# The gate stage of a two-block network: high and low halves of four matmul units side by side in PSUM, and the scaling moved to GpSimd

## The chip, the cores and the metric

The kernel runs on one core of a Trainium2 chip. One program computes the whole network in one launch. The metric is the device time of one execution in microseconds (us). An execution carries five instruction streams that meet only at semaphores: TensorE (PE, matmul and weight load), VectorE (DVE), ScalarE (ACT), GpSimd (POOL) and SyncE (SP, which here only issues DMAs).

## The reference, cut to what matters

The network is two blocks of two layers each, on 256 tokens of width 1024, all in float32. The change lies in the first mixer of the first layer, a gated MLP:

```python
def gmlp_mixer(x, w_in, ln_g, ln_b, w_s, b_s, w_out):
    B, S, _ = x.shape
    z = jax.nn.gelu(x @ w_in)
    u, v = z[..., :GMLP_WIDTH], z[..., GMLP_WIDTH:]
    v = layernorm(v, ln_g, ln_b)
    v = v.reshape(B, S // GMLP_CHUNK, GMLP_CHUNK, GMLP_GROUPS, GMLP_GROUP_DIM)
    ...
    v = jnp.einsum('gpq,bnqgc->bnpgc', ws, v) + b_s.T[None, None, :, :, None]
    return (u * v.reshape(B, S, GMLP_WIDTH)) @ w_out

    y = rmsnorm(h, norm_g[layer, 0])
    y = gmlp_mixer(y, ...)
    h = h + rmsnorm(y, norm_g[layer, 1])
    y = rmsnorm(h, norm_g[layer, 2])
    y = conv_ffn(y, ...)
```

The first RMS norm is applied late: the matmuls run on the unscaled input, and their results are multiplied by the token's `rs2` (one over the root mean square) afterwards.

## The kernel before

**Tiling.** All weights come as units of 128 x 2048 floats (1 MB), in the order in which they are used. SP loads unit u into slot u % 3 of `raw`, as soon as the low part of unit u-3 is made. Each unit is split in two: ACT copies it to a rounded high part `w_hi` (`split_hi`, 2048 columns), and DVE subtracts that from the raw unit and leaves the low part `w_lo` (`split_lo`). Activations are held in the same two parts, `a_hi` and `a_lo`, side by side in `a_hl`. A product is the sum of three matmuls: high x high, high weight x low activation, low weight x high activation.

**The stage.** Units 0 to 3 make v (token-major, in the `acc` banks of PSUM), units 4 to 7 make u (feature-major, each unit two tiles of 128 features x 256 tokens, in the `wk` banks), units 8 to 11 are the output projection (into `wk` again). The four units of u are numbered q = 0 to 3 below. On PE the order is: unit 3, u units q = 0, 1, 2, then `spatial` (the einsum with w_s), then q = 3, then unit 8, whose second token half may write banks 2 and 3 of `wk` only once the last unit of u has been read out of them (`last_bank`), then units 9 to 11 (`last_downs`).

**How a u unit runs.** `unit_feat` (L693) issues for each of 8 slices and 2 feature tiles the three matmuls of `three` (L687 to L691), all of 256 columns, into one PSUM bank: 48 matmuls. It starts when the low weights are there. DVE's `scale_u(q)` (L2030) multiplies that bank by `rs2` into `uT`, ACT's `gelu_u(q)` (L1500) applies gelu to `uT` in place, and DVE's `gate(b)` (L2034) adds the spatial bias to a bank of `acc` (L2039) and multiplies by `uT` (L2044). ACT's `gate_high` and DVE's `gate_low` make the high and low parts `b_hi`, `b_lo` for the projection. Elsewhere in the kernel a second form of unit exists: `unit_pair` (L706), which streams `a_hl` as 512 columns (high and low activations side by side) past the high weights, two banks wide, 16 matmuls, and then `low_pair` (L754), 16 matmuls of 256 columns with the low weights. There ACT copies the low halves of the two banks to SBUF (L1542) and DVE adds the high halves to them (L2079).

**What sets the order.** Every engine's order is written out by hand. DVE's order in this stage is `norm_v` (layer norm of v, with `split_lo` of unit 6 in it), then three times `scale_u` with `split_lo` of units 7 and 8 between, then the gates, `split_lo` of unit 9, `scale_u(3)` and the rest. POOL has nothing to compute in the stage: after a memset it waits until unit 4 is done and loads the two gain rows (`load_gains`, L572) that DVE multiplies by in the stage that follows (L1795). After the stage POOL takes part in the FFN's gating: `gate_first` (L393, both inputs in SBUF) and `gate_second` (L401).

Of the kernel before, what the change touches and what calls it, by code (L numbers as in the profile page):

```python
# [122 lines left out]
def build(nc, xT, x_rows, gains, cols, rows, ws, wsT, rel_bias, pool_w, onehot, line_dram, lines_dram, out):  # L123
    ctx = ExitStack()
    with ctx:
# [146 lines left out]
        v_gelu, u_scaled, u_gelu = sem("v_gelu"), sem("u_scaled"), sem("u_gelu")  # L272
# [18 lines left out]
        d_low, s_low = sem("d_low"), sem("s_low")  # L291
# [12 lines left out]
                ("pad_zero", "low", "padded", "tap2", "taps", "gelu", "gated", "hid_hi", "hid_lo", "last_gated", "last_lo")} for l in range(2)]  # L304
# [247 lines left out]
        def _(pool):  # L552
# [133 lines left out]
        def _(pe):  # L686
# [1777 lines left out]
```

## Time and profile before

| what | value |
|---|---|
| time, median of 3 runs | 1054.45 us (1054.29 to 1055.08) |
| the profiled execution's own time | 1055.49 us |
| its span, first to last instruction | 1053.8 us |
| PE busy in the span | 1044.0 us (99%) |
| DVE busy | 783.9 us (74%) |
| ACT busy | 614.5 us (58%) |
| POOL busy | 119.2 us (11%) |
| the changed stage in the span | about 31 to 81 us |

The profiled execution is 1.0 us above the median, and 1.7 us of it lie outside the span. Matmuls are pipelined, so that records overlap: a 512-column matmul is recorded with 0.39 us, but the next one starts 0.23 us later. Costs of PE are therefore read from start to start. DVE's records overlap a little too (0.69 us recorded for a 512-column addition, the next starts after 0.60 us).

### The profile page before, as it was taken

What the parts mean: (1) busy time and instruction counts of PE and PEld (TensorE: products, weight loads), DVE (VectorE), ACT (ScalarE), POOL (GpSimd) and SP (SyncE); (2) the same over time, 40 slices, a digit from 0 to 9 for tenths busy, and PEclk for the clock granted to TensorE, in tenths of its full rate; (3) what the DMA queues carried; (4) which work ended last, traced back from release to release, by engine and by line L of the source; (5) the groups of instructions that cost most, each with busy time, mean ns of one, the idle gap of its engine ahead of it and who ended that gap; (6) DMA issues with size and microseconds to landing.
All of it is one profiled execution on the core that took longest, in us unless ns stands there. A gap on an engine that the chain in (4) does not pass through costs nothing.

```text
span 1053.8 us, 15320 instructions
## 1 busy us (share of the span) xinstructions
PE 1044.0 (99%) x6158; PEld 919.5 (87%) x6158; DVE 783.9 (74%) x960; ACT 614.5 (58%) x846; POOL 119.2 (11%) x117
## 2 busy tenths in 40 slices
PE   9999999999999999999999999999999999999997
PEld 7989888888999898888888988888899989888886
DVE  6979877676888799788868856556878869655654
ACT  6757666557666676665766535344566666434442
POOL 0000431220000004753110000000000000000000
PEclk9999999999999999999999999999999999999999
DMA  8944885554445447756551564555354435665551
GB/s 312 346 156 173 285 302 170 190 203 157 165 157 198 160 159 242 266 187 236 171 200 40 208 249 163 204 196 173 147 208 153 138 105 198 221 211 187 184 175 40
DMA packets 31750, 201.17 MB, mean 191 GB/s; under 512 B 3736, under 2 KB 4416, under 8 KB 9408
## 3 DMA queue, kind: packets, MB, share of 16 engines
q1 hardware_dynamic: 28608, 188.12, 50.4%
q0 software_dynamic: 3072, 12.07, 3.5%
q8 instruction: 49, 0.80, 0.3%
q14 instruction: 21, 0.17, 0.0%
HBM read 199.12 MB, written 2.63 MB: 191 GB/s over the span
## 4 chain that ended last, share of the span: by engine, by line
PE 92%; DVE 3%; DMA 2%; ACT 1%; issue 1%; SPq 0%; DVEq 0%; ACTq 0%
PE wk L713 22%; PE wk L761 15%; PE acc L689 9%; PE acc L690 9%; PE acc L691 9%; PE wk L689 5%; PE wk L691 5%; PE wk L690 5%; PE wk L742 4%; PE wk L831 2%; DMA raw<-ws 2%; PE acc L742 2%; PE acc L761 1%; PE acc L927 1%; PE acc L1213 0%
## 5 line engine op out<-in xcount | busy, mean ns | idle before, releaser
L354 DVE TENSOR_TENSOR w_lo<-raw,w_hi 128x2048 fp32r<-128x2048 f32 x159 | 365.5, 2303 | 46.2 <-ACT w_hi L333 41.2
L333 ACT ACTIVATE w_hi<-raw 128x2048 fp32r<-128x2048 f32 x165 | 314.5, 1908 | 9.7 <-DMA raw<-ws 7.2
L713 PE MATMUL wk<-a_hl,w_hi 128*128 128x512 f32 x1024 | 243.2, 390 | 0.0
L713 PEld LDWEIGHTS wk<-a_hl,w_hi 128*128 128x128 f32 x1024 | 190.6, 188 | 38.5
L761 PEld LDWEIGHTS wk<-a_hl,w_lo 128*128 128x128 f32 x1296 | 165.3, 191 | 5.5
L689 PE MATMUL acc<-w_hi,b_hl 128*128 128x512 f32 x432 | 168.9, 391 | 0.0
L690 PE MATMUL acc<-w_lo,b_hl 128*128 128x512 f32 x432 | 168.6, 390 | 0.0
L691 PE MATMUL acc<-w_hi,b_hl 128*128 128x512 f32 x432 | 168.1, 389 | 0.0
L761 PE MATMUL wk<-a_hl,w_lo 128*128 128x256 f32 (+1 forms) x1296 | 168.0, 283 | 0.0
L1687 ACT ACTIVATE region<-wk 128x512 f32<-128x512 f32 x30 | 17.9, 596 | 158.1 <-PE wk L761 158.1
L691 PEld LDWEIGHTS acc<-w_hi,b_hl 128*128 128x128 f32 x432 | 81.1, 188 | 17.2
L689 PEld LDWEIGHTS acc<-w_hi,b_hl 128*128 128x128 f32 x432 | 81.3, 188 | 15.7
L690 PEld LDWEIGHTS acc<-w_lo,b_hl 128*128 128x128 f32 x432 | 81.3, 188 | 15.2
L2262 DVE TENSOR_TENSOR region<-wk,region 128x512 f32<-128x512 f32 x30 | 20.7, 691 | 92.8 <-ACT region L1687 92.8
L2089 DVE SCALAR_TENSOR_TENSOR region<-region,prm 128x256 f32<-128x256 f32 x176 | 82.0, 508 | 7.2 <-ACT region L1554 5.7
L393 POOL TENSOR_TENSOR region<-region 128x512 f32<-128x512 f32 x20 | 50.7, 2537 | 233.2 <-ACT region L1583 233.2
L1542 ACT ACTIVATE region<-wk 128x512 f32<-128x512 f32 x42 | 25.0, 594 | 73.5 <-PE wk L761 73.5
L1554 ACT ACTIVATE region<-region,prm 128x256 f32<-128x256 f32 x88 | 47.7, 590 | 8.5 <-DVE region L2079 8.5
L2079 DVE TENSOR_TENSOR region<-wk,region 128x512 f32<-128x512 f32 x42 | 28.8, 687 | 28.1 <-ACT region L1542 28.0
L1350 ACT ACTIVATE b_hl<-region 128x512 fp32r<-128x512 f32 x58 | 36.0, 623 | 22.3 <-POOL region L393 9.2
L578 POOL DMA_DIRECT2D gain<-gains x12 | 6.9, 577 | 371.0 <-ACT region L1477 183.1
L742 PE MATMUL wk<-a_hl,w_hi 128*128 128x256 f32 x352 | 45.4, 284 | 0.9 <-DVE a_hl L1887 0.8
(287 smaller groups left out, 1538.9 us busy)
## 6 DMA issues: line engine op xcount, KB each, us to landing
raw<-ws SPq DMA_DIRECT2D x171, 1024.0 KB, 4.9
gain<-gains POOLq DMA_DIRECT2D x12, 512.0 KB, 6.0
raw<-ws SPq DMA_DIRECT2D x12, 256.0 KB, 6.6
region<-rows SPq DMA_DIRECT2D x1, 1664.0 KB, 10.9
lines_dram<-line_dram POOLq DMA_DIRECT2D x1, 1536.0 KB, 8.2
bias<-gains POOLq DMA_DIRECT2D x3, 512.0 KB, 8.1
region<-xT SPq DMA_DIRECT2D x4, 256.0 KB, 6.4
x<-x_rows SPq DMA_DIRECT2D x1, 1024.0 KB, 9.2
```

The costliest lines, as they stand in the source:

```text
L333: act.activation(high_of(u), raw[:, u % RAW, :], ACT.Copy).then_inc(hi_ready, 1)
L354: dve.tensor_tensor(low_of(u), raw[:, u % RAW, :], high_of(u).bitcast(F32), ALU.subtract).then_inc(lo_ready, 1)
L393: eng.tensor_tensor(hf[:, p:p + 2, :], gl[:, p:p + 2, :], cv[:, p:p + 2, 1, :], ALU.mult)\
L689: pe.matmul(o, still, moving, start=first, stop=False, skip_group_check=True)
L690: pe.matmul(o, still, moving_lo, start=False, stop=False, skip_group_check=True)
L691: return pe.matmul(o, still_lo, moving, start=False, stop=last, skip_group_check=True)
L713: pe.matmul(banks[:, m, :], wh[:, k, m * P:(m + 1) * P], a_hl[:, k, :, :].rearrange("p e t -> p (e t)"), start=k == 0, stop=False, skip_gr ...
L742: pe.matmul(banks[:, m, :].rearrange("p (e t) -> p e t", e=2)[:, :, c], wh[:, k, m * P:(m + 1) * P], a_hl[:, k, :, c], start=h == 0 and k ...
L761: mm = pe.matmul(banks[:, m, T + c.start:2 * T], wl[:, k, m * P:(m + 1) * P], hi[:, k, c], start=False, stop=k == DT - 1, skip_group_check ...
L1350: act.activation(dst, src, ACT.Copy, **kw).then_inc(done, 1)
L1554: act.activation(cv[:, p + a, q, :], hb[:, p + a, q, 2:HW], ACT.Identity, scale=w, bias=bb)\
L2089: dve.scalar_tensor_tensor(out=cv[:, p + a, q, :], in0=hb[:, p + a, q, tap:tap + T], scalar=prm[:, bass.ds(col, 1)], in1=cv[:, p + a, q, : ...
```

## The change

Each u unit now runs as `unit_pair`: 16 matmuls of 512 columns and 16 of 256 instead of 48 of 256. The results lie in two half banks: the first 256 columns of each of two banks hold the products with the high activations and with the low weights, the other 256 those with the low activations. Units q = 0 and 2 use banks 0 and 1 of `wk`, q = 1 and 3 banks 2 and 3, so that q = 2 and 3 have to wait until q = 0 and 1 are read out. ACT copies the low halves into `gain`, which serves as scratch (`copy_u`), DVE adds the high halves to them into `uT` (`sum_u`), and the multiplication by `rs2` becomes an instruction of its own on `uT` in SBUF: on POOL for q = 0 to 2, on DVE for q = 3. The two gain rows are loaded only when the scratch is free, after the fourth sum. In `norm_v`, `split_lo` of unit 6 moves between the first two instructions, and `split_lo` of units 7 and 8 follow the second and the third sum. ACT's copies are placed between its splits, and `gate_high` of bank 0 comes ahead of `gelu_u(2)`. Renamed semaphores elsewhere change no order.

```diff
+        def u_banks(q):
+            return wk[:, 2 * (q % 2):2 * (q % 2) + 2, :]
+
+        def u_copied(q):
+            return two(gain[:, q % 2, 0:2 * T])
...
             pool.memset(wst[HD:P, :, 0:HD], 0.0).then_inc(wst_masked, 1)
-            pool.wait_ge(unit_done, U_GMLP + 5)
+            pool.wait_ge(wst_masked, 1)
+            pool.wait_ge(rs2_ready, 1)
+            for q in range(3):
+                pool.wait_ge(u_summed, q + 1)
+                pool.tensor_tensor(uT[:, 2 * q:2 * q + 2, :], uT[:, 2 * q:2 * q + 2, :], rs2_two, ALU.mult).then_inc(u_scaled, 1)
+            pool.wait_ge(u_summed, 4)
             load_gains(J_GMLP)
...
             for q in range(4):
-                if q == 2:
+                if q == 1:
                     pe.wait_ge(line_copied, 1)
-                if q == 3:
                     pe.wait_ge(sd2_ready, 1)
-                unit_feat(U_GMLP + 4 + q, q)
+                elif q >= 2:
+                    pe.wait_ge(u_summed, q - 1)
+                unit_pair(U_GMLP + 4 + q, u_banks(q))
...
             pe.wait_ge(gate_lo, 1)
-            unit_down(U_GMLP + 8, *b_pair(0), True, res=wk, last_bank=(u_scaled, 4))
+            pe.wait_ge(u_summed, 3)
+            unit_down(U_GMLP + 8, *b_pair(0), True, res=wk, last_bank=(u_summed, 4))
...
+            act.wait_ge(unit_done, U_GMLP + 5)
+            act.activation(u_copied(0), u_banks(0)[:, :, T:2 * T], ACT.Copy).then_inc(u_low, 1)
             split_hi(act, U_GMLP + 3 + CUT)
...
+            def copy_u(q):
+                act.wait_ge(unit_done, U_GMLP + 4 + q + 1)
+                act.activation(u_copied(q), u_banks(q)[:, :, T:2 * T], ACT.Copy).then_inc(u_low, 1)
...
-            for q in range(3):
-                split_hi(act, U_GMLP + 4 + q + CUT)
-                gelu_u(q)
-            for b in range(3):
-                gate_high(b)
+            copy_u(1)
+            split_hi(act, U_GMLP + 4 + CUT)
+            gelu_u(0)
+            split_hi(act, U_GMLP + 5 + CUT)
+            copy_u(2)
+            gelu_u(1)
+            split_hi(act, U_GMLP + 6 + CUT)
+            gate_high(0)
+            gelu_u(2)
+            gate_high(1)
+            gate_high(2)
+            copy_u(3)
             split_hi(act, U_GMLP + 7 + CUT)
             gelu_u(3)
...
-                split_lo(dve, U_GMLP + 3 + CUT)
+                    if n == 0:
+                        split_lo(dve, U_GMLP + 3 + CUT)
...
-            def scale_u(q):
-                dve.wait_ge(unit_done, U_GMLP + 4 + q + 1)
-                dve.tensor_tensor(uT[:, 2 * q:2 * q + 2, :], two(wk[:, q, :]), rs2_two, ALU.mult).then_inc(u_scaled, 1)
+            def sum_u(q):
+                dve.wait_ge(u_low, q + 1)
+                dve.tensor_tensor(uT[:, 2 * q:2 * q + 2, :], u_banks(q)[:, :, 0:T], u_copied(q), ALU.add).then_inc(u_summed, 1)
...
+            sum_u(0)
             norm_v()
-            for q in range(3):
-                scale_u(q)
-                if q < 2:
-                    split_lo(dve, U_GMLP + 4 + q + CUT)
+            for q in range(1, 3):
+                sum_u(q)
+                split_lo(dve, U_GMLP + 3 + q + CUT)
             gate(0)
...
             split_lo(dve, U_GMLP + 6 + CUT)
-            scale_u(3)
+            sum_u(3)
+            dve.wait_ge(u_summed, 4)
+            dve.wait_ge(u_scaled, 3)
+            dve.tensor_tensor(uT[:, 6:8, :], uT[:, 6:8, :], rs2_two, ALU.mult).then_inc(u_scaled, 1)
             gate_low(2)
```

VectorE from the layer norm of v to the first gate, before (L2032 is `scale_u`, L354 `split_lo`; `region` holds `uT` and v):

```order
L2012 SCALAR_TENSOR_TENSOR region<-region 128x1024 [waits row_landed,ln_step]
L2012 SCALAR_TENSOR_TENSOR region<-region 128x1024
L354 TENSOR_TENSOR w_lo<-raw,w_hi 128x2048 [waits unit_done,hi_ready]
L2017 RECIPROCAL region<-region 128x2 [waits ln_sd_ready]
L2020 SCALAR_TENSOR_TENSOR region<-region 128x1024 [waits ln_step]
L2020 SCALAR_TENSOR_TENSOR region<-region 128x1024
L2032 TENSOR_TENSOR region<-wk,region 128x512 [waits unit_done]
L354 TENSOR_TENSOR w_lo<-raw,w_hi 128x2048 [waits unit_done,hi_ready]
L2032 TENSOR_TENSOR region<-wk,region 128x512 [waits unit_done]
L354 TENSOR_TENSOR w_lo<-raw,w_hi 128x2048 [waits unit_done,hi_ready]
L2032 TENSOR_TENSOR region<-wk,region 128x512 [waits unit_done]
L2039 TENSOR_TENSOR bias<-acc,region 128x512 [waits spatial_done]
```

VectorE at the same place after the change (L2061 is `sum_u`, L356 `split_lo`; `gain` is the scratch):

```order
L2061 TENSOR_TENSOR region<-wk,gain 128x512 [waits u_low]
L2040 SCALAR_TENSOR_TENSOR region<-region 128x1024 [waits row_landed,ln_step]
L356 TENSOR_TENSOR w_lo<-raw,w_hi 128x2048 [waits unit_done,hi_ready]
L2040 SCALAR_TENSOR_TENSOR region<-region 128x1024
L2046 RECIPROCAL region<-region 128x2 [waits ln_sd_ready]
L2049 SCALAR_TENSOR_TENSOR region<-region 128x1024 [waits ln_step]
L2049 SCALAR_TENSOR_TENSOR region<-region 128x1024
L2061 TENSOR_TENSOR region<-wk,gain 128x512 [waits u_low]
L356 TENSOR_TENSOR w_lo<-raw,w_hi 128x2048 [waits unit_done,hi_ready]
L2061 TENSOR_TENSOR region<-wk,gain 128x512 [waits u_low]
L356 TENSOR_TENSOR w_lo<-raw,w_hi 128x2048 [waits unit_done,hi_ready]
L2068 TENSOR_TENSOR bias<-acc,region 128x512 [waits spatial_done]
```

The first sum stands ahead of the layer norm, each sum waits for ACT's copy instead of for PE, and the number of instructions up to the first gate is the same.

GpSimd from its constants to its first gating instruction, before:

```order
L569 MEMSET minus_half 128x4
L583 MEMSET region 64x8x64 [waits row_landed,consts_set]
L578 DMA gain<-gains 128x1024 [waits unit_done]
L578 DMA gain<-gains 128x1024
L393 TENSOR_TENSOR region<-region 128x512 [waits ffn0_gelu,ffn0_taps]
```

GpSimd after the change (L596 is the scaling, L586 `load_gains`):

```order
L577 MEMSET minus_half 128x4
L591 MEMSET region 64x8x64 [waits row_landed,consts_set]
L596 TENSOR_TENSOR region<-region 128x512 [waits u_summed,rs2_ready,wst_masked]
L596 TENSOR_TENSOR region<-region 128x512 [waits u_summed] x2
L586 DMA gain<-gains 128x1024 [waits u_summed]
L586 DMA gain<-gains 128x1024
```

Three multiplications with both inputs in SBUF stand ahead of the gain loads, and the loads wait for the fourth sum instead of for unit 4.

## Rows read from the trace of the kernel before

**Rows 1.** The page: busy time, share and instructions; the chain by engine.

```profile
PE 1044.0 (99%) x6158; PEld 919.5 (87%) x6158; DVE 783.9 (74%) x960; ACT 614.5 (58%) x846; POOL 119.2 (11%) x117
PE 92%; DVE 3%; DMA 2%; ACT 1%; issue 1%; SPq 0%; DVEq 0%; ACTq 0%
```

**Rows 2.** Timeline of PE, 31 to 62: start us, us, engine, line, operation, [idle before].

```profile
31.22 0.39 PE L691 MATMUL acc<-w_hi,a_hl 128*128 128x512 f32 x1
31.75 0.38 PE L689 MATMUL wk<-a_hl,w_hi 128*128 128x256 f32 x1
31.97 0.28 PE L690 MATMUL wk<-a_hl,w_hi 128*128 128x256 f32 x1
32.09 0.28 PE L691 MATMUL wk<-a_hl,w_lo 128*128 128x256 f32 x1
...
49.12 3.73 PE L980 MATMUL acc<-region 128*128 128x128 f32 x32
52.61 0.36 PE L689 MATMUL wk<-a_hl,w_hi 128*128 128x256 f32 x1
...
58.44 0.40 PE L689 MATMUL wk<-w_hi,b_hl 128*128 128x512 f32 x1
...
61.19 0.39 PE L689 MATMUL wk<-w_hi,b_hl 128*128 128x512 f32 x1
```

**Rows 3.** Timeline of VectorE, 29 to 60, same columns.

```profile
29.40 2.29 DVE L354 TENSOR_TENSOR w_lo<-raw,w_hi 128x2048 fp32r<-128x2048 f32 x1
...
38.01 2.48 DVE L2012 SCALAR_TENSOR_TENSOR region<-region 128x1024 f32<-128x1024 f32 x2
...
45.20 0.69 DVE L2032 TENSOR_TENSOR region<-wk,region 128x512 f32<-128x512 f32 x1
45.80 2.29 DVE L354 TENSOR_TENSOR w_lo<-raw,w_hi 128x2048 fp32r<-128x2048 f32 x1
...
53.51 0.69 DVE L2049 TENSOR_TENSOR b_hl<-bias,b_hl 128x512 fp32r<-128x512 f32 x1 [0.70 <-ACT b_hl L1350]
...
59.58 0.68 DVE L2032 TENSOR_TENSOR region<-wk,region 128x512 f32<-128x512 f32 x1
```

**Rows 4.** Timeline of PE, 99.6 to 106: one unit in pair form, and the next one's start.

```profile
99.66 3.82 PE L713 MATMUL wk<-a_hl,w_hi 128*128 128x512 f32 x16
103.32 2.08 PE L761 MATMUL wk<-a_hl,w_lo 128*128 128x256 f32 x16
105.23 1.09 PE L713 MATMUL wk<-a_hl,w_hi 128*128 128x512 f32 x4
```

**Rows 5.** The page's groups of the copy and the sum: xcount | busy, mean ns | idle before.

```profile
L1542 ACT ACTIVATE region<-wk 128x512 f32<-128x512 f32 x42 | 25.0, 594 | 73.5 <-PE wk L761 73.5
L2079 DVE TENSOR_TENSOR region<-wk,region 128x512 f32<-128x512 f32 x42 | 28.8, 687 | 28.1 <-ACT region L1542 28.0
```

**Rows 6.** Timelines of GpSimd and VectorE where both work: at 103, 432 and 462.

```profile
103.23 1.29 POOL L393 TENSOR_TENSOR region<-region 128x512 f32<-128x512 f32 x1 [63.92 <-ACT region L1583]
103.49 3.18 DVE L354 TENSOR_TENSOR w_lo<-raw,w_hi 128x2048 fp32r<-128x2048 f32 x1
...
432.51 2.55 POOL L393 TENSOR_TENSOR region<-region 128x512 f32<-128x512 f32 x1 [1.09 <-ACT region L1583]
431.62 2.28 DVE L354 TENSOR_TENSOR w_lo<-raw,w_hi 128x2048 fp32r<-128x2048 f32 x1
433.83 0.68 DVE L2079 TENSOR_TENSOR region<-wk,region 128x512 f32<-128x512 f32 x1
...
462.54 2.54 POOL L393 TENSOR_TENSOR region<-region 128x512 f32<-128x512 f32 x1 [7.49 <-ACT region L1583]
461.65 2.29 DVE L354 TENSOR_TENSOR w_lo<-raw,w_hi 128x2048 fp32r<-128x2048 f32 x1
463.85 2.39 DVE L2130 TENSOR_TENSOR o_lo_t<-region,o_hi_t 128x512 fp32r<-128x512 f32 x2
```

**Rows 7.** GpSimd's gain loads (line L578: issue to landing), and VectorE's first use of them.

```profile
DMA to landing us min/median/max: 4.4/6.0/10.8
71.73 0.15 DVE L1792 TENSOR_SCALAR ss_eps<-ss 128x1 f32<-128x1 f32 x1 [4.01 <-ACT region L1382]
```

**Rows 8.** Stretches at the span's end: us, PE, PEld, DVE, ACT, POOL busy (x), PEclk, DMA.

```profile
1040.00:1048.00 8.00, 7.95 (x36) 6.24 (x34) 2.84 (x7) 1.51 (x6) 0.00 (x0) 1.00 0.18 66
1048.00:1051.00 3.00, 0.00 (x0) 0.00 (x0) 2.36 (x7) 0.97 (x3) 0.00 (x0) 1.00 0.04 15
1051.00:1053.80 2.80, 0.00 (x0) 0.00 (x0) 0.17 (x1) 0.00 (x0) 0.00 (x0) 0.51 0.52 172
```

More of the change, by code:

```diff
@@ L270, in build @@
         out_stored = sem("out_stored")
-        v_gelu, u_scaled, u_gelu = sem("v_gelu"), sem("u_scaled"), sem("u_gelu")
+        v_gelu, u_low, u_summed, u_scaled, u_gelu = (
+            sem("v_gelu"), sem("u_low"), sem("u_summed"), sem("u_scaled"), sem("u_gelu"))
         ln_step, ln_sd_ready, spatial_done = sem("ln_step"), sem("ln_sd_ready"), sem("spatial_done")
@@ L289, in build @@
             sem("o_hi"), sem("o_lo"), sem("sub_ready"))
-        d_low, s_low = sem("d_low"), sem("s_low")
+        qk_low = sem("qk_low")
+        pad_zero = sem("pad_zero")
         sq_ready, sk_ready, sv_ready = sem("sq_ready"), sem("sk_ready"), sem("sv_ready")
@@ L303, in build @@
         ffn = [{n: sem(f"ffn{l}_{n}") for n in
-                ("pad_zero", "low", "padded", "tap2", "taps", "gelu", "gated", "hid_hi", "hid_lo", "last_gated", "last_lo")} for l in range(2)]
+                ("low", "padded", "tap2", "taps", "gelu", "gated", "hid_hi", "hid_lo", "last_gated", "last_lo")} for l in range(2)]
         mlp = [{n: sem(f"mlp{l}_{n}") for n in
@@ L1637, in diff_outputs @@
                     part(2 * j + 1)
-            low_copy(U_DIFF, wk[:, 0:2, :], diff_low[:, 0, :, :], d_low)
+            low_copy(U_DIFF, wk[:, 0:2, :], diff_low[:, 0, :, :], qk_low)
             split_hi(act, U_DIFF + 3)
-            low_copy(U_DIFF + 1, wk[:, 2:4, :], diff_low[:, 1, :, :], d_low)
+            low_copy(U_DIFF + 1, wk[:, 2:4, :], diff_low[:, 1, :, :], qk_low)
             split_hi(act, U_DIFF + 4)
@@ L1728, in _ @@
             act.preload_act_table_set("natural_log_exp_and_others")
-            low_copy(U_STICK, wk[:, 0:2, :], stick_low[:, 0, :, :], s_low)
+            low_copy(U_STICK, wk[:, 0:2, :], stick_low[:, 0, :, :], qk_low)
             split_hi(act, U_STICK + 3)
-            low_copy(U_STICK + 1, wk[:, 2:4, :], stick_low[:, 1, :, :], s_low)
+            low_copy(U_STICK + 1, wk[:, 2:4, :], stick_low[:, 1, :, :], qk_low)
             split_hi(act, U_STICK + 4)
             act.wait_ge(sq_ready, 1)
-            low_copy(U_STICK + 2, acc[:, 2:4, :], stick_low[:, 0, :, :], s_low)
+            low_copy(U_STICK + 2, acc[:, 2:4, :], stick_low[:, 0, :, :], qk_low)
             split_hi(act, U_STICK + 5)
@@ L2133, in ffn_phase @@
             def ffn_phase(l, base, n):
-                dve.memset(hb[:, :, :, 0:2], 0.0).then_inc(ffn[l]["pad_zero"], 1)
-                dve.wait_ge(ffn[l]["pad_zero"], 1)
+                dve.memset(hb[:, :, :, 0:2], 0.0).then_inc(pad_zero, 1)
+                dve.wait_ge(pad_zero, l + 1)
                 for i in range(FI):
@@ L2210, in _ @@
             dve.wait_ge(lam_step, 5)
-            feat_sum(wk[:, 0:2, :], diff_low[:, 0, :, :], d_low, 1, qT[:, 0:2, :], dq_ready)
+            feat_sum(wk[:, 0:2, :], diff_low[:, 0, :, :], qk_low, 1, qT[:, 0:2, :], dq_ready)
             split_lo(dve, U_DIFF + 3)
-            feat_sum(wk[:, 2:4, :], diff_low[:, 1, :, :], d_low, 2, kT[:, 0:2, :], dk_ready)
+            feat_sum(wk[:, 2:4, :], diff_low[:, 1, :, :], qk_low, 2, kT[:, 0:2, :], dk_ready)
             diff_bias(0)
@@ L2332, in stick_rest @@
                     stick_low_part(t)
-            feat_sum(wk[:, 0:2, :], stick_low[:, 0, :, :], s_low, 1, qT[:, 0:2, :], sq_ready)
+            feat_sum(wk[:, 0:2, :], stick_low[:, 0, :, :], qk_low, 3, qT[:, 0:2, :], sq_ready)
             split_lo(dve, U_STICK + 3)
-            feat_sum(wk[:, 2:4, :], stick_low[:, 1, :, :], s_low, 2, qT[:, 2:4, :], sq_ready)
-            feat_sum(acc[:, 2:4, :], stick_low[:, 0, :, :], s_low, 3, qT[:, 4:6, :], sq_ready)
+            feat_sum(wk[:, 2:4, :], stick_low[:, 1, :, :], qk_low, 4, qT[:, 2:4, :], sq_ready)
+            feat_sum(acc[:, 2:4, :], stick_low[:, 0, :, :], qk_low, 5, qT[:, 4:6, :], sq_ready)
             for c in range(3, 12):
```

## The prediction

> **What bounds the kernel now.** I read the page first: PE is busy for 1044.0 of 1053.8 us, and 92% of the chain that ended last is PE [rows 1]. Whatever PE gains in a stage is therefore kept, unless PE then waits, and whatever PE waits for in a stage is lost. So I went to PE's timeline of the stage: it has no gap between 31.75 and 81, apart from one at its start. The last matmul of unit 3 starts at 31.22 and, at the 0.23 us from start to start of 512-column matmuls, the next could have started at 31.45; the first u unit starts at 31.75, right behind DVE's low part of unit 4, which ends at 29.40 + 2.29 = 31.69 [rows 2, 3]. Then I laid DVE's timeline beside it, because the change hangs PE on DVE more closely. DVE is just as full: from 38.01, where the layer norm of v begins, to 60.26, where the last scaling ends (59.58 + 0.68), it has one idle stretch of note, 0.70 us ahead of the first `gate_low` [rows 3]. PE needs that last scaling for the second half of unit 8, which starts at 61.19 [rows 2], so DVE is only 0.93 us early there. This is the place where the change is decided.
>
> **PE's part.** A u unit in the old form is 48 matmuls at 0.12 us from start to start [rows 2], 5.76 us. In the pair form the trace shows one unit from 99.66 to the next one's start at 105.23, 5.57 us [rows 4]. That is 0.19 us a unit, 0.76 us for four. The pair form waits for the high weights only, which were there long before, so the gap of 0.30 us at 31.45 goes as well, and with it the slow restart of the first matmul (0.22 us to the next instead of 0.12). In sum PE arrives earlier by 0.76 + 0.30 + 0.10, about 1.2 us. Laid out: q = 0 from 31.45, q = 1 from 37.0, q = 2 from 42.6, `spatial` from 48.2 (3.49 us as before, 49.12 to 52.61 [rows 2]), q = 3 from 51.7, unit 8 from 57.2 instead of 58.44, and its second half would start 2.75 us later (58.44 to 61.19), at 60.0.
>
> **ACT's part.** Four copies are added, 0.59 us each [rows 5]. They stand on ACT's queue, which has room in this stage; the first of them waits for unit 4 until 37.2 and pushes `split_hi` of unit 6 from 35.2 to 37.7, so DVE's `split_lo` of it may start from 39.7, which is about where DVE arrives. The last copy stands behind `gate_high(2)`, and can be done by 59.9 by the layout below; DVE asks for it at 61.5. I cost ACT at nothing; without that cover the fourth copy's 0.59 us would come on top.
>
> **DVE's part without GpSimd.** `scale_u` (0.69 us) becomes `sum_u` (0.69 us [rows 5]); the first of them moves ahead of the layer norm, where ACT's copy is done at 37.8, just before DVE is free at 38.0. The multiplication for q = 3 (0.6 us) is added, but behind the fourth sum, which is what PE waits for. So up to the end of the fourth sum DVE has the same work as before, and would end it at 60.26.
>
> **GpSimd's three multiplications.** Here the trace of before has a close relative: L393, the same 128x512 multiplication of float32 in SBUF. Alone it takes 1.29 us, but beside DVE's `split_lo` 2.54 us [rows 6]. At 462.54 it begins while a `split_lo` runs, and ends at 465.08, 1.14 us behind that instruction's end (461.65 + 2.29 = 463.94). DVE's next instruction, also with two SBUF inputs, is held: two of them take 2.39 us from 463.85, where two take about 1.29. At 103.23 GpSimd was first, and the `split_lo` took 3.18 us instead of 2.29. So GpSimd waits for the instruction that DVE has under way, and then DVE's next instruction with two SBUF inputs waits for GpSimd, up to 1.1 us. An addition with one input in PSUM is not held: 0.68 us at 433.83, while GpSimd was still at work until 435.06 [rows 6].
>
> The Trainium skill's page "GPSIMD Engine Reference", section "Key points", says that GpSimd shares its SBUF interfaces with VectorE and contends with instructions that have two SBUF inputs. By that rule `sum_u` and the first half of a gate, which read PSUM, go free, and the trace agrees with its 0.68 us.
>
> Each multiplication is released by the sum in front, and DVE is fully loaded behind each:
> - The first waits for the first layer-norm instruction (to 39.8) and holds `split_lo` of unit 6 until 41.0: 1.10 us lost.
> - The second waits for `split_lo` of unit 7 (to 49.7) and holds until 50.9. DVE spends 0.60 us of that on the third sum, which goes free; `split_lo` of unit 8 loses about 0.50.
> - The third waits for `split_lo` of unit 8 (to 53.0) and holds until 54.2. The gate's PSUM half goes free, its SBUF half loses about 0.35.
>
> Together 1.95 us. The fourth sum starts at 59.58 + 1.95 = 61.5 and ends at 62.2.
>
> **The sum.** PE stands at unit 8's second half from 60.0 and goes on at 62.28 (0.06 us behind DVE, as at 31.69 to 31.75), with 0.08 us of restart. Before, this half started at 61.19. The stage is later by 62.28 + 0.08 - 61.19, some 1.1 us: PE's 1.2 us are gone, and 1.1 more. What follows on PE has its inputs: `split_lo` of units 9, 10 and 11 ends at 61.5, 67.0 and 69.8, PE wants them at 65.1, 67.8 and 70.5. From there all moves together, since the next stage begins with this one's result.
>
> The span becomes 1053.8 + 1.1 = 1054.9, that execution's own time 1055.49 + 1.1 = 1056.6, and the median 1054.45 + 1.1 = 1055.5 us.
>
> **The gain rows.** They are issued at about 62.3 and 62.9 instead of 38. At the median landing of 6.0 us they are there at 69, at the maximum of 10.8 at 73.7; DVE first needs them at 71.73 + 1.1 = 72.8, after 4 us of idleness [rows 7]. I take the median: nothing; the other end is 0.9 us.
>
> **Rivals.**
> - *GpSimd gives way* (its multiplications find gaps, or DVE is held for less than the rows show). The fourth sum ends at 60.26, PE goes on at 60.32 + 0.08 and the stage is 0.8 us earlier: 1053.65. For it speaks only that the scaling's second input is a broadcast row, which L393 has not; against it three collisions in [rows 6].
> - *GpSimd holds every DVE instruction*, sums and PSUM halves too, so that each of the three costs 1.1 us: 3.3 us. The fourth sum ends at 63.6, PE goes on at 63.6 + 0.14, the stage is 2.5 us later: 1056.95, slower by more than 0.2%. It decides from 3.0 us of hold in all on. Against it speaks the 0.68 us row. The same time would come of a multiplication that takes 0.5 us longer with the broadcast row.
> - *The gains land late*: 0.4 to 0.9 us on top of the forecast, 1056.2.
> - *The clock*. PE's wait of 2.3 us would be the longest inside the span. At the tail the granted clock was still 1.00 in the first 3 us without a matmul, and fell to 0.51 on average (1.2 GHz) in the last 2.8 us [rows 8]. So the forecast's wait should leave it; a wait over 3 us, as in the second rival, might not: three us of work at half speed after it would be 1.5 us on top of that rival, 1058.5.
> - *The fourth copy or the wait for q = 0's sum holds PE*: both have over 1 us of slack in the layout, and count for nothing here.
>
> **How the numbers follow.** The forecast has 0.70, GpSimd giving way 0.15, holding everything 0.08, late gains 0.05, a fallen clock 0.02. A measurement of this kernel can tell about 0.2%, 2.1 us, from no change. The forecast, the first and the third rival lie within that (0.90, less 0.01 for a part of the first that goes further); the second and the fourth lie above (0.10 together). Range: the first rival's 1053.65 less 0.35 for the spread of the runs, to the second's 1056.95: 1053.3 to 1057.0.
>
> **What would show it.** After the change, PE should start u units at about 31.45, 37.0, 42.6 and 51.7, and wait some 2.3 us ahead of unit 8's second half for DVE's fourth sum. GpSimd's three multiplications should be recorded with about 2.3, 3.3 and 3.3 us, and of DVE's instructions `split_lo` of unit 6 with 3.4, of unit 8 with 2.8 and the first gate's second half with 1.0 us, against 2.29, 2.29 and 0.69. The prediction is wrong in its main step if these are recorded at their old lengths, or if PE waits elsewhere in the stage.

## The result, and the profile after

The changed kernel takes 1057.49 us in the median (before, on the same chip: 1054.52); the ratio is 1.0027, with a 95% interval of 1.0018 to 1.0036. Run again beside the kernel before, it took 1057.67 against 1054.67: 1.0023 (1.0013 to 1.0033). So it is slower by a quarter of a percent. The forecast was 1055.5, and its range ended at 1057.0.

The nine times of the second measurement are the first clue, because they fall into two groups: 1055.37, 1055.67 and 1055.85, then 1057.29 to 1058.50 (six). The lower group is the forecast's time.

Two of the nine times of the first measurement, 1284.14 and 1473.05 us, come from executions whose mean granted clock was 0.75 and 0.65; the ratio leaves them out (the median of the other seven is 1057.42 us), and since the profile of that measurement is of the first of them, the profiles below are from three later executions of the changed kernel. They took 1057.29 us (called X), 1055.57 (Y) and 1057.61 (Z): one of the lower group and two of the upper.

On the page of X the answers to [rows 1] show hardly a change. PE's busy time is 0.2 us less, POOL's 8.8 more, and the chain has gained one percent of DVE.

```profile
PE 1043.8 (99%) x6094; PEld 916.9 (87%) x6094; DVE 786.5 (75%) x961; ACT 616.7 (58%) x850; POOL 128.0 (12%) x120
PE 92%; DVE 4%; issue 1%; ACT 1%; DMA 1%; SPq 0%; DVEq 0%; ACTq 0%
```

PE's timeline of Y, the answer to [rows 2] (start, length, line, [idle before]):

```profile
30.68 3.79 PE L726 MATMUL wk<-a_hl,w_hi 128*128 128x512 f32 x16
...
36.22 3.82 PE L726 MATMUL wk<-a_hl,w_hi 128*128 128x512 f32 x16
...
41.78 3.82 PE L726 MATMUL wk<-a_hl,w_hi 128*128 128x512 f32 x16
...
59.00 0.39 PE L704 MATMUL wk<-w_hi,b_hl 128*128 128x512 f32 x1
61.31 0.50 PE L702 MATMUL wk<-w_hi,b_hl 128*128 128x512 f32 x1 [1.92 <-DVE region L2061]
```

The units of u are 5.54 and 5.56 us apart, as forecast (5.57), and PE's one wait in the stage is where it was forecast: ahead of unit 8's second half, for the fourth sum. From start to start PE is ready at 59.00 + 0.23 = 59.23 and goes on at 61.31, 2.08 us later; the forecast said 2.3.

DVE's and GpSimd's timelines of Y, the answers to [rows 3] and [rows 6]:

```profile
38.86 3.37 DVE L356 TENSOR_TENSOR w_lo<-raw,w_hi 128x2048 fp32r<-128x2048 f32 x1
...
46.54 2.28 DVE L356 TENSOR_TENSOR w_lo<-raw,w_hi 128x2048 fp32r<-128x2048 f32 x1
48.74 0.68 DVE L2061 TENSOR_TENSOR region<-wk,gain 128x512 f32<-128x512 f32 x1
49.34 2.76 DVE L356 TENSOR_TENSOR w_lo<-raw,w_hi 128x2048 fp32r<-128x2048 f32 x1
52.02 0.68 DVE L2068 TENSOR_TENSOR bias<-acc,region 128x512 f32<-128x512 f32 x1
52.73 1.07 DVE L2073 TENSOR_TENSOR bias<-bias,region 128x512 f32<-128x512 f32 x1
...
60.57 0.69 DVE L2061 TENSOR_TENSOR region<-wk,gain 128x512 f32<-128x512 f32 x1
```

```profile
37.92 2.16 POOL L596 TENSOR_TENSOR region<-region 128x512 f32<-128x512 f32 x1 [8.72 <-DVE region L2061]
46.70 6.55 POOL L596 TENSOR_TENSOR region<-region 128x512 f32<-128x512 f32 x2 [6.62 <-DVE region L2061]
```

The three holds are there at the forecast's sizes: `split_lo` of unit 6 at 3.37 us, of unit 8 at 2.76, the first gate's SBUF half at 1.07, while the third sum and the gate's PSUM half go free at 0.68.

The windows show where Y and X part. The columns are those of [rows 8]; the third from the end is the granted clock. Y:

```profile
61.00:62.00 1.00, 0.69 (x3) 0.60 (x4) 0.96 (x3) 0.00 (x0) 0.44 (x1) 1.00 0.86 139
62.00:63.00 1.00, 1.00 (x6) 0.82 (x5) 1.00 (x2) 0.99 (x2) 0.84 (x2) 1.00 0.55 197
63.00:64.00 1.00, 1.00 (x6) 0.81 (x5) 0.97 (x3) 1.00 (x1) 0.00 (x0) 1.00 1.01 426
```

X:

```profile
61.00:62.00 1.00, 0.61 (x3) 0.51 (x4) 0.96 (x3) 0.00 (x0) 0.36 (x1) 1.00 0.85 131
62.00:63.00 1.00, 1.00 (x5) 0.79 (x4) 1.00 (x3) 0.91 (x2) 0.92 (x2) 0.87 0.50 147
63.00:64.00 1.00, 1.00 (x4) 0.78 (x3) 0.96 (x3) 1.00 (x1) 0.00 (x0) 0.50 0.93 393
64.00:65.00 1.00, 1.00 (x4) 0.81 (x3) 1.00 (x1) 1.00 (x2) 0.00 (x0) 0.50 0.94 389
65.00:66.00 1.00, 1.00 (x3) 0.72 (x3) 1.00 (x1) 0.98 (x2) 0.00 (x0) 0.50 0.57 184
66.00:67.00 1.00, 1.00 (x5) 0.83 (x4) 1.00 (x3) 0.99 (x3) 0.00 (x0) 0.92 0.80 262
```

In X the granted clock falls to 0.50 (1.2 of 2.4 GHz) behind the wait and stays there until it rises again between 66 and 67. PE's timeline of X shows the same in its matmuls:

```profile
61.39 0.50 PE L702 MATMUL wk<-w_hi,b_hl 128*128 128x512 f32 x1 [1.92 <-DVE region L2061]
...
62.44 0.40 PE L703 MATMUL wk<-w_lo,b_hl 128*128 128x512 f32 x1
62.67 0.55 PE L704 MATMUL wk<-w_hi,b_hl 128*128 128x512 f32 x1
63.02 0.63 PE L702 MATMUL wk<-w_hi,b_hl 128*128 128x512 f32 x1
63.45 0.63 PE L703 MATMUL wk<-w_lo,b_hl 128*128 128x512 f32 x1
```

PE is back at work at 61.39, and the first slow matmul starts at 62.67; from 63.02 on they start 0.43 us apart instead of 0.23. The wait in front of it is 1.92 us in X and in Y. They are the same code, with the same holds and the same wait, and X is 1.72 us longer.

### The profile page after: what moved, and what is told of

Its sections match the earlier page's. It is cut to its first block, busy times and chain, and to the rows that moved or that the text cites. A ratio compares the mean times of both kernels' runs of the same rounds, so it can differ in the third digit from the quotient of the medians.

```text
span 1282.4 us, 15203 instructions
## 1 busy us (share of the span) xinstructions
PE 1274.5 (99%) x6094; PEld 1016.8 (79%) x6094; DVE 793.0 (62%) x961; ACT 617.2 (48%) x850; POOL 132.4 (10%) x120
## 4 chain that ended last, share of the span: by engine, by line
PE 99%; DVE 0%; ACT 0%; issue 0%; DVEq 0%; POOL 0%; POOLq 0%
PE wk L726 24%; PE wk L774 15%; PE acc L704 11%; PE acc L702 10%; PE acc L703 10%; PE wk L704 4%; PE wk L702 4%; PE wk L755 4%; PE wk L703 4%; PE wk L844 2%; PE acc L755 2%; PE acc L774 1%; PE acc L940 1%; PE wk L964 0%; PE wk L947 0%; PE acc L1228 0%
## 5 line engine op out<-in xcount | busy, mean ns | idle before, releaser
L356 DVE TENSOR_TENSOR w_lo<-raw,w_hi 128x2048 fp32r<-128x2048 f32 x159 | 366.7, 2310 | 96.9 <-ACT w_hi L335 50.8
L726 PE MATMUL wk<-a_hl,w_hi 128*128 128x512 f32 x1088 | 320.2, 456 | 0.0
L726 PEld LDWEIGHTS wk<-a_hl,w_hi 128*128 128x128 f32 x1088 | 215.4, 200 | 86.4
L774 PEld LDWEIGHTS wk<-a_hl,w_lo 128*128 128x128 f32 x1360 | 203.3, 212 | 13.1
L774 PE MATMUL wk<-a_hl,w_lo 128*128 128x256 f32 (+1 forms) x1360 | 207.7, 314 | 0.0
L702 PE MATMUL acc<-w_hi,b_hl 128*128 128x512 f32 x432 | 197.4, 457 | 0.0
L703 PE MATMUL acc<-w_lo,b_hl 128*128 128x512 f32 x432 | 197.1, 456 | 0.0
L704 PE MATMUL acc<-w_hi,b_hl 128*128 128x512 f32 x432 | 196.9, 456 | 0.0
L704 PEld LDWEIGHTS acc<-w_hi,b_hl 128*128 128x128 f32 x432 | 86.1, 199 | 35.5
L703 PEld LDWEIGHTS acc<-w_lo,b_hl 128*128 128x128 f32 x432 | 86.8, 201 | 33.2
L702 PEld LDWEIGHTS acc<-w_hi,b_hl 128*128 128x128 f32 x432 | 86.1, 199 | 33.2
L395 POOL TENSOR_TENSOR region<-region 128x512 f32<-128x512 f32 x20 | 57.4, 2872 | 244.7 <-ACT region L1611 244.7
L755 PE MATMUL wk<-a_hl,w_hi 128*128 128x256 f32 x352 | 52.9, 314 | 0.7 <-DVE a_hl L1915 0.7
L586 POOL DMA_DIRECT2D gain<-gains x12 | 7.0, 582 | 446.9 <-ACT region L1492 224.7
L755 PEld LDWEIGHTS wk<-a_hl,w_hi 128*128 128x128 f32 x352 | 51.5, 217 | 1.8 <-issue 1.0
```

Of the source, the lines that this page charges most:

```text
L356: dve.tensor_tensor(low_of(u), raw[:, u % RAW, :], high_of(u).bitcast(F32), ALU.subtract).then_inc(lo_ready, 1)
L395: eng.tensor_tensor(hf[:, p:p + 2, :], gl[:, p:p + 2, :], cv[:, p:p + 2, 1, :], ALU.mult)\
L702: pe.matmul(o, still, moving, start=first, stop=False, skip_group_check=True)
L703: pe.matmul(o, still, moving_lo, start=False, stop=False, skip_group_check=True)
L704: return pe.matmul(o, still_lo, moving, start=False, stop=last, skip_group_check=True)
L726: pe.matmul(banks[:, m, :], wh[:, k, m * P:(m + 1) * P], a_hl[:, k, :, :].rearrange("p e t -> p (e t)"), start=k == 0, stop=False, skip_gr ...
```

## The experiments

Three theories stood against each other. **A**: the three holds cost the forecast's 1 us, and the second group of times is chance that has nothing to do with the change. **B**: the wait that they make lets the clock fall, in a part of the executions. **C**: the longer times come from the chip of the first measurement, not from the kernel.

**The changed kernel again** (label e1_after; no edit).

> The changed kernel once more, for a profile at full clock. Theory A (the stage alone): three holds of GpSimd add 1.95 us to VectorE's chain, PE waits 2.3 us ahead of unit 8's second half, and the time is 1.1 us above before, with a mean granted clock of 0.999 as before. Theory B (the wait brings the clock down): in part of the executions PE's granted clock falls to 1.2 GHz for some us behind that wait; the mean clock is then 0.998 to 0.995 and the time 1 to 4 us above theory A's, differently from run to run. Theory C (the chip of that measurement): the low mean clocks have nothing to do with the kernel; before shows them on this chip too, or after shows none.

Measured: the second measurement above. Theory C falls, since the kernel before ran at 1054.67 beside it, and both kinds of times came from one chip.

**Without GpSimd's multiplications** (e2_no_pool). Three quarters of u are then not scaled.

```diff
                 pool.wait_ge(u_summed, q + 1)
-                pool.tensor_tensor(uT[:, 2 * q:2 * q + 2, :], uT[:, 2 * q:2 * q + 2, :], rs2_two, ALU.mult).then_inc(u_scaled, 1)
+                pool.memset(minus_half[:, q:q + 1], -0.5).then_inc(u_scaled, 1)
```

> The changed kernel with GpSimd's three multiplications left out (u is not scaled by rs2 for its first six tiles; a 128x1 memset counts the semaphore instead). Theories A and B: no hold, the fourth sum ends at 60.3 in the span, PE waits 0.3 us ahead of unit 8's second half, and the time is 0.8 us below before with a clock of 0.999 in every run. Theory C: 0.8 us below before plus whatever the chip's clock takes, as much as in the changed kernel.

Measured: 1054.50 us (1054.00 to 1054.67 in 11 runs, one group), ratio 0.9997 (0.9988 to 1.0006). DVE's timeline has all lengths back:

```profile
38.87 2.29 DVE L356 TENSOR_TENSOR w_lo<-raw,w_hi 128x2048 fp32r<-128x2048 f32 x1
...
48.19 0.69 DVE L2061 TENSOR_TENSOR region<-wk,gain 128x512 f32<-128x512 f32 x1 [0.45 <-ACT gain L1519]
48.80 2.28 DVE L356 TENSOR_TENSOR w_lo<-raw,w_hi 128x2048 fp32r<-128x2048 f32 x1
...
59.18 0.68 DVE L2061 TENSOR_TENSOR region<-wk,gain 128x512 f32<-128x512 f32 x1
```

The `split_lo` of unit 6 starts at the same time as in execution Y, so the fourth sums can be compared: 59.18 here, 60.57 there, 1.39 us. That is the holds' 1.94 less 0.55 us, most of it the 0.45 that DVE now waits for ACT's third copy. The second group of times goes when the multiplications go, and so does the 1 us. But against the kernel before only 0.17 us is won, not 0.8; PE still waits here:

```profile
59.92 0.50 PE L702 MATMUL wk<-w_hi,b_hl 128*128 128x512 f32 x1 [0.52 <-DVE region L2061]
```

**The wait filled** (e3_filled). PE multiplies a constant tile in the time in which it would wait; the delay stays, the idleness goes.

```diff
                     if last_bank is not None and h == 1:
+                        keep_warm(acc[:, 0, 0:T], filled)
                         pe.wait_ge(*last_bank)
...
-            unit_down(U_GMLP + 8, *b_pair(0), True, res=wk, last_bank=(u_summed, 4))
+            unit_down(U_GMLP + 8, *b_pair(0), True, res=wk, last_bank=(u_summed, 4), filled=16)
```

> The changed kernel with 16 matmuls of 256 bf16 columns on constants, into a bank that is free, between the two halves of unit 8: PE is at work for some 1.9 of the 2.3 us in which it waits. The holds stay. Theory A: time as the changed kernel, 1.1 us above before. Theory B: no drop of the clock, 0.999 in every run, 1.1 us above before while the changed kernel is 2 to 5 us above. Theory C: the same spread of clock and time as the changed kernel.

Measured: 1055.76 us (1055.49 to 1056.45 in 11 runs, one group), ratio 1.0011 (1.0002 to 1.0020). The holds are those of Y (3.37, 2.77, 1.07 us) and PE goes on at 61.12, nearly as late as in Y. PE's timeline:

```profile
59.03 1.92 PE L965 MATMUL acc<-warm 128*128 128x256 bf16 x16
61.12 0.50 PE L702 MATMUL wk<-w_hi,b_hl 128*128 128x512 f32 x1 [0.16 <-DVE region L2062]
```

Useless work of PE makes the changed kernel 1.9 us faster in the median. This is what theory B demands and theory A excludes.

**The wait alone, in the kernel before** (e4_before_late; e7_before_late2 with 256 in place of 1024 columns in the second addition). DVE gets two idle additions ahead of the last scaling; nothing of the change is in these kernels.

```diff
             split_lo(dve, U_GMLP + 6 + CUT)
+            for idle, n in ((o_lo_t, 2048), (o_hi_t, 1024)):
+                dve.tensor_tensor(idle[:, 0:n // T, :], row[:, 0:n].rearrange("p (k t) -> p k t", t=T), row[:, 0:n].rearrange("p (k t) -> p k t", t=T), ALU.add)
             scale_u(3)
```

> The kernel before with two idle additions on VectorE (2048 and 1024 columns, 3.35 us) ahead of the last scaling, which is what PE waits for at unit 8's second half: PE waits some 2.5 us there, without pair form, without GpSimd. Theories A and C: 2.5 us above before, clock 0.999. Theory B: 2.5 us plus a drop of the clock in part of the runs, so 3.5 to 6.5 us above before, with a mean clock of 0.998 to 0.995 and a spread of 1 us or more.

> The kernel before with two idle VectorE additions of 2048 and 256 columns ahead of its last scaling of u, so that TensorE waits about 1.9 us at unit 8's second half, as in the changed kernel, with GpSimd idle there. Theory B: times in two groups, about 1056.7 without a fall of the clock and 1058.4 with one, granted clock at 0.50 for some 3 us after the wait in the latter. Theory A: 1056.7 in every run, full clock.

Measured, e4: 1057.53, 1057.53, 1058.29, 1058.85, 1058.86. Its profiled execution is one of the two fastest, with a wait of 2.74 us and a clock of 1.00 behind it:

```profile
63.30 0.50 PE L689 MATMUL wk<-w_hi,b_hl 128*128 128x512 f32 x1 [2.74 <-DVE region L2032]
```

e7: 1056.61, 1056.83 and 1056.93, one at 1057.64, then 1058.38 to 1059.09 (four). Its profiled execution is the slowest; the wait is 1.90 us, and the clock is at 0.50 right behind it:

```profile
63.22 0.64 PE L689 MATMUL wk<-w_hi,b_hl 128*128 128x512 f32 x1 [1.90 <-DVE region L2032]
```

```profile
63.00:64.00 1.00, 0.78 (x2) 0.67 (x3) 1.00 (x3) 0.81 (x2) 0.00 (x0) 0.71 0.97 410
64.00:65.00 1.00, 1.00 (x4) 0.73 (x3) 0.96 (x2) 1.00 (x1) 0.00 (x0) 0.50 0.14 57
```

So a wait of 1.90 us was followed by a fall of the clock without GpSimd at work and without pair units; by the grouping of the times, not in every execution.

**The same, filled** (e8_late_filled: e4 and 22 of the matmuls of e3).

```diff
-            unit_down(U_GMLP + 8, *b_pair(0), True, res=wk, last_bank=(u_scaled, 4))
+            unit_down(U_GMLP + 8, *b_pair(0), True, res=wk, last_bank=(u_scaled, 4), filled=22)
```

> The kernel before with the idle additions of 2048 and 1024 columns, and with 22 bf16 matmuls of 256 columns on TensorE in the wait that they make. The delay stays, the idle time goes. Theory B: 1057.5 in every run, the fastest of the runs with the same additions and nothing in the wait, clock 1.00 behind it. Theory A: the same two groups as without the matmuls, 1057.5 and 1058.9.

Measured: 1057.50 us; five of seven runs lie within 1057.22 to 1057.76, two are at 1058.20 and 1058.54. In the profile the fill takes the place of the wait, and the clock is 1.00 behind it:

```profile
60.52 2.57 PE L952 MATMUL acc<-warm 128*128 128x256 bf16 x22
63.20 0.50 PE L689 MATMUL wk<-w_hi,b_hl 128*128 128x512 f32 x1
```

```profile
64.00:65.00 1.00, 1.00 (x6) 0.83 (x5) 0.96 (x3) 1.00 (x1) 0.00 (x0) 1.00 0.00 0
```

By times alone this tells less than was expected of it, since two runs lie where e4's upper ones lie. Neither is profiled, but their mean granted clocks are on record, 0.999 and 1.000, against 0.997 or 0.998 in each profiled execution with a fall (0.998 to 1.000 in those without). So it is probably not a fall that makes these two late; what does is not known.

**The fourth sum ahead** (e5_sum_first): DVE makes it before `split_lo` of unit 9, ACT its copy before `gate_high(2)`.

```diff
-            gate_high(2)
             copy_u(3)
+            gate_high(2)
...
-            split_lo(dve, U_GMLP + 6 + CUT)
             sum_u(3)
+            split_lo(dve, U_GMLP + 6 + CUT)
```

> The changed kernel with the fourth sum of u put ahead of unit 9's low split on VectorE, and the fourth copy ahead of the next gate's on ScalarE: TensorE should reach unit 8's second half (near 59.9 us) with the sum done, and wait instead some 1.4 us at unit 10 for its low part. Theory B (a wait of nearly 2 us lets the clock fall, a shorter one does not): 1055.0 us, one group of times, granted clock 0.999. Theory A (the three holds cost 1 us and the clock is chance): the same spread as the changed kernel, 1055.4 to 1058.5, less the 0.5 us of wait saved. If the clock falls for a wait of 1.4 us as well, the wait stays in unit 10 and the time is 1056.5 to 1058.

Measured: 1055.29 us (1055.08 to 1056.05 in 11 runs, one group), ratio 1.0003 (0.9995 to 1.0012). The wait has moved to unit 10 and is shorter:

```profile
59.61 0.50 PE L702 MATMUL wk<-w_hi,b_hl 128*128 128x512 f32 x1 [0.18 <-DVE region L2061]
...
66.63 0.47 PE L702 MATMUL wk<-w_hi,b_hl 128*128 128x512 f32 x1 [1.29 <-DVE w_lo L356]
```

Two lines in another order bring the ratio from 1.0023 to 1.0003, some 2.1 us: the wait is not gone, but no run shows the second group.

**DVE scales** (e6_dve_scales): all four multiplications on DVE, each right behind its sum.

```diff
-            for q in range(3):
-                pool.wait_ge(u_summed, q + 1)
-                pool.tensor_tensor(uT[:, 2 * q:2 * q + 2, :], uT[:, 2 * q:2 * q + 2, :], rs2_two, ALU.mult).then_inc(u_scaled, 1)
...
             sum_u(0)
+            scale_u(0)
             norm_v()
             for q in range(1, 3):
                 sum_u(q)
+                scale_u(q)
                 split_lo(dve, U_GMLP + 3 + q + CUT)
...
```

> The changed kernel with the four multiplications by the gain on VectorE, each right behind its sum; GpSimd only loads the gains. VectorE has three more operations of about 0.6 us ahead of the wait (1.8 us) in place of the holds (1.1, 0 and 0.5 us that the changed kernel's profile shows). Theory B: TensorE waits 1.8 to 2.1 us at unit 8's second half, and the times lie in two groups, about 1055.6 and 1057.5. Theory A: 1055.6 in all runs. If GpSimd's holds are what is special, and not the length of the wait, the time is that of the kernel without them, 1054.5.

Measured: 1057.60 us, ratio 1.0021 (1.0012 to 1.0030), in two groups: 1055.81 to 1056.45 (four) and 1057.33 to 1058.12 (seven). PE's timeline and a window behind it:

```profile
61.77 0.50 PE L699 MATMUL wk<-w_hi,b_hl 128*128 128x512 f32 x1 [2.51 <-DVE region L2058]
```

```profile
64.00:65.00 1.00, 1.00 (x3) 0.74 (x3) 1.00 (x2) 1.00 (x2) 0.00 (x0) 0.50 0.94 393
```

With no GpSimd beside DVE the result is the same as that of the change. GpSimd's holds are nothing special: some 1.8 us of DVE's own work (three multiplications at 0.61 us from start to start) do the same. Moving the multiplications off DVE has bought nothing that can be measured.

**One multiplication on GpSimd** (e9_one_pool: e5, with the first and the third multiplication on DVE; `scale_u` as in e6, waiting for the one before it).

```diff
-            for q in range(3):
-                pool.wait_ge(u_summed, q + 1)
-                pool.tensor_tensor(uT[:, 2 * q:2 * q + 2, :], uT[:, 2 * q:2 * q + 2, :], rs2_two, ALU.mult).then_inc(u_scaled, 1)
+            pool.wait_ge(u_summed, 2)
+            pool.wait_ge(u_scaled, 1)
+            pool.tensor_tensor(uT[:, 2:4, :], uT[:, 2:4, :], rs2_two, ALU.mult).then_inc(u_scaled, 1)
...
             sum_u(0)
+            scale_u(0)
             norm_v()
...
+            split_lo(dve, U_GMLP + 5 + CUT)
+            scale_u(2)
...
```

> The kernel with the fourth sum first, and the first and third multiplication on VectorE besides, so that GpSimd keeps the second alone, the one that held nothing. VectorE gives 0.6 us each for two multiplications and is spared the holds of 1.1 and of 0.5 plus 0.4 us, so TensorE's waits in units 8 and 10 should go from 1.47 to about 0.7 us: 1054.5 us, one group of times, full clock, against 1054.95 of the kernel before. If the holds came from any multiplication on GpSimd wherever it lies, it stays at 1055.3.

Measured: 1055.28 us, ratio 1.0004 (0.9995 to 1.0013): no better than e5. PE's wait in unit 10 is 1.19 us, where 0.7 was expected (e5: 1.29). The expectation took the wrong multiplication for the harmless one:

```profile
49.20 2.77 DVE L356 TENSOR_TENSOR w_lo<-raw,w_hi 128x2048 fp32r<-128x2048 f32 x1
```

```profile
46.72 3.10 POOL L596 TENSOR_TENSOR region<-region 128x512 f32<-128x512 f32 x1 [16.93 <-DVE region L2061]
```

The second multiplication runs until 49.82, waits for the `split_lo` in front of it and holds the one behind it, as the prediction had it. DVE saves no more than 0.41 us up to its fourth sum (58.46 here, 58.87 in e5), and 0.27 of that lies ahead of its first sum (37.33 against 37.60). No version that computes the whole result is faster than the kernel before by more than can be measured.

**Three more profiled executions** (e10_look and e11_look, the changed kernel; e12_before_look, the kernel before).

> The changed kernel, one more profiled execution. Theory B: either TensorE's clock falls to 0.50 for some 3 us behind the wait at unit 8's second half and the time is 1057.3 to 1058.5, or it does not and the time is 1055.4 to 1055.9; the wait itself, near 1.9 us, is the same in both. Theory A: the two groups of times differ somewhere else in the span.

> The changed kernel, one further profiled execution, with the same two outcomes: a fall of the clock with 1057.3 to 1058.5, or none with 1055.4 to 1055.9.

> The kernel before, a second profiled execution. TensorE's gap of 0.30 us ahead of unit 4 of u, which the first profile showed and the prediction credited to the pair form, should be absent if it is not typical, and VectorE's slack at unit 8's second half then about 0.5 us, not 0.93; if the gap is typical, both are as in the first profile.

e10 and e11 are the executions Y and Z above. In Z the wait is 2.51 us, not 1.92, and the clock falls as in X (windows and PE's timeline of Z):

```profile
62.00:63.00 1.00, 1.00 (x5) 0.80 (x6) 1.00 (x2) 0.45 (x1) 0.90 (x2) 0.92 0.90 139
63.00:64.00 1.00, 1.00 (x4) 0.81 (x3) 0.96 (x3) 1.00 (x2) 0.38 (x1) 0.50 0.90 369
```

```profile
61.85 0.50 PE L702 MATMUL wk<-w_hi,b_hl 128*128 128x512 f32 x1 [2.51 <-DVE region L2061]
```

DVE is later there from the start of the stage: ACT makes the high part of unit 5 at 31.98, where X has 31.23, after a longer wait for the weights. So the expectation that the wait is the same in all executions was wrong. ACT's timelines of Z and of X:

```profile
31.98 1.92 ACT L335 ACTIVATE w_hi<-raw 128x2048 fp32r<-128x2048 f32 x1 [2.49 <-DMA raw<-ws]
```

```profile
31.23 1.92 ACT L335 ACTIVATE w_hi<-raw 128x2048 fp32r<-128x2048 f32 x1 [2.04 <-DMA raw<-ws]
```

The second profile of the kernel before (1055.00 us) shows PE without the gap of [rows 2] at 31.45, and DVE's last scaling just ahead of PE:

```profile
31.35 0.40 PE L691 MATMUL acc<-w_hi,a_hl 128*128 128x512 f32 x1
31.59 0.28 PE L689 MATMUL wk<-a_hl,w_hi 128*128 128x256 f32 x1
...
60.94 0.39 PE L689 MATMUL wk<-w_hi,b_hl 128*128 128x512 f32 x1
```

```profile
59.77 0.68 DVE L2032 TENSOR_TENSOR region<-wk,region 128x512 f32<-128x512 f32 x1
```

DVE ends at 60.45 and is 0.49 us early, not 0.93.

**All profiled executions together.** If only the end of the wait and the clock matter, then an execution's time less the start of unit 8's second half must be one number without a fall of the clock, and another with one.

| kernel | PE's wait, us | second half starts | clock fell | time, us | difference |
|---|---|---|---|---|---|
| before, first profile | 0 | 61.19 | no | 1055.49 | 994.30 |
| before, e12 | 0 | 60.94 | no | 1055.00 | 994.06 |
| e2 | 0.52 | 59.92 | no | 1054.15 | 994.23 |
| e3, filled | 0.16 | 61.12 | no | 1055.49 | 994.37 |
| e8, filled | 0 | 63.20 | no | 1057.43 | 994.23 |
| changed, Y | 1.92 | 61.31 | no | 1055.57 | 994.26 |
| e4 | 2.74 | 63.30 | no | 1057.53 | 994.23 |
| changed, X | 1.92 | 61.39 | yes | 1057.29 | 995.90 |
| changed, Z | 2.51 | 61.85 | yes | 1057.61 | 995.76 |
| e6 | 2.51 | 61.77 | yes | 1057.60 | 995.83 |
| e7 | 1.90 | 63.22 | yes | 1059.09 | 995.87 |

Seven executions without a fall have 994.06 to 994.37, four with one 995.76 to 995.90. (e5 and e9 wait later; their unit 10, which follows 24 matmuls or 5.44 us behind the second half where nothing waits, starts at 66.63 and 66.22, which gives 994.32 both times, at 1055.51 and 1055.10.) The fall costs 995.84 - 994.24 = 1.6 us, in each of the four: X, Z and e6, which have the change, and e7, which is the kernel before with a wait put in. Behind the start of that second half nothing else moves the time by more than 0.3 us in these executions.

The mean granted clock that every execution has on record agrees for those without a profile: it is 0.997 or 0.998 in every run of the upper groups of e1, e6 and e7, and 0.998 to 1.000 in the lower ones. The value 0.998 occurs on both sides, so a single run can't be sorted by it alone. The run of e7 at 1057.64 has 1.000 and thus belongs to the lower group.

## Why the prediction was wrong

**What held.** PE's gain in a unit, 0.19 us, was right (0.20 to 0.22 in Y), as were the three holds with their sizes (1.08, 0.48 and 0.38 us against 1.10, 0.50 and 0.35), GpSimd's 2.16 us and 6.55 for two (forecast 2.3 and 3.3 each), the place of the one wait, and its length to 0.2 us. The gain rows, issued at 61.56, hold nothing up: in execution Y DVE's first instruction that uses them follows the one before it without idle time. Where the clock stays up, the time is the forecast's: 1055.37 to 1055.85 in the measurement with a median of 1054.67 before, 0.7 to 1.2 us more, forecast 1.1. Within the stage the forecast holds too: from the start of unit 4 to that of unit 8's second half Y takes 30.63 us (30.68 to 61.31), the two profiles of before 29.44 and 29.35, which is 1.2 to 1.3 us more. The forecast had 1.4 there (31.45 to 62.28 against 31.75 to 61.19) and took off 0.3 for an earlier start of unit 4.

The Trainium skill's page "GPSIMD Engine Reference", section "Key points", on contention with two SBUF inputs, agrees with the holds again: 1.07 us for the gate's SBUF half against 0.68 for its PSUM half just ahead of it.

**The step that failed** is the rival on the clock: "So the forecast's wait should leave it; a wait over 3 us, as in the second rival, might not", with a chance of 0.02. It rested on [rows 8], one stretch at the span's end where the clock was still 1.00 in 3 us without a matmul. Those rows show one execution; in Y the same stretch, 1048 to 1051, has a granted clock of 0.87, so that the clock fell earlier there. Here waits of 1.90 and 1.92 us brought the clock down in two executions and left it in a third, two of 2.51 us brought it down, and one of 2.74 us left it. A single row says what can happen, not what always does. The price that the rival gave a fall, 1.5 us, was near the 1.6 measured, though no row showed its three us at half speed; its condition and its chance were wrong. Of the nine times of the second measurement six lie in the upper group, so the likeliest outcome was the forecast's mechanism and 1.6 us on top, 1055.5 + 1.6 = 1057.1; where DVE is later as in Z, some 0.5 us more. The measured 1057.49 and 1057.67 lie near there. Four of the six lie higher, at 1058.26 to 1058.50, and the first measurement has 1059.04 and 1060.23 as well, the latter with a mean granted clock of 0.995, lower than any profiled execution here; what these have on top is not shown.

The Trainium skill's page "TensorE: Matmul & The Clock Gate", section "HAM oscillation — how this bites in real kernels", tells of a kernel in which each wait for data lowers the clock and the cost comes anew every time. The trace agrees in part: a wait was followed by a fall and cost 1.6 us in X, Z, e6 and e7, and by none in Y and e4. The same section names, as what lowers the clock, a longer gap than the 1.90 to 2.51 us in those four; the measurement decides. The page also says, in the section "What's actually happening", that what the chip judges PE's activity by runs freely and does not start anew with a kernel, so that the moment at which the clock rises varies. If the same holds for the fall, it would explain why X and Y part; no run here shows it.

**Other terms mis-sized.** The 0.30 us gap and 0.10 us of restart that PE was to win are not there in the second profile of before, whose unit 4 follows at 0.24 us. Unit 4 does start earlier with the change, but for another reason, which is open (below), so that this part of the sum came out by luck. The profile of before was an execution 1.0 us above the median with a late start of the stage (unit 4 at 31.75; Y has 30.68), and DVE's slack in it was 0.93 us where 0.49 was seen later. The forecast's moments are therefore all 0.8 to 1.0 us late (31.45 and 62.28 against 30.68 and 61.31), on PE and DVE alike, which cancels in the sum. It does not help the rival "GpSimd gives way": that has 0.8 us, and e2 showed 0.17. Two terms of it are off: the 0.30 us gap was not there to be won, and without the holds DVE waits 0.45 us for ACT's third copy, where the prediction counted ACT at nothing. Behind the holds that wait does not appear (the third sum of Y starts right behind `split_lo`), so that the forecast's sum was spared this term by luck.

**What stays open.** Which of two executions with the same wait loses its clock was not settled: X and Y show the same work and the same wait in the stage up to 62.6 us. Nor was what makes the upper two runs of e8 late, and the highest ones of the changed kernel. Unit 4 starts at 30.48 to 30.89 in the eight profiles with pair units used here but at 31.01 to 31.81 in the five without; the cause is open, but it lies ahead of the stage, since ACT's fourth copy of weights, behind a wait for a DMA, already starts at 8.65 to 9.68 us in the eight and at 9.68 to 10.58 in the five.

## What to carry to other kernels

A wait of PE that is new in the middle of a span has two prices, its length and what the clock does behind it; here 1 us of delay came with 1.6 us lost to half speed in most runs, so ask of each change whether it makes one long wait out of slack, and prefer shorter ones (up to 1.29 us left the clock up here) or an order that moves the awaited instruction forward (two lines here). When times fall into two groups, profile one execution of each before explaining the median. And a multiplication moved to GpSimd is not free for DVE: count what it holds (1.94 us for three here), against the 0.6 us each that DVE would have needed.

## What was unexpected

The fall does not come during the wait in any of the four profiles that show one. PE has worked for 1.28 us in X (61.39 to 62.67) when its matmuls turn slow, but in e7 they are slow from the first one behind the wait. A longer wait doesn't always bring it: 2.74 us left the clock at 1.00 in e4's profile. The shorter waits of 1.19 and 1.29 us (e9, e5) left it there in both profiles, with no upper group in 22 runs. A fill of 16 matmuls on a constant tile, 1.92 us of work that computes nothing, was worth 1.9 us in the median.
